# Latents' queries inside the expert stage's first tile, with groups of two choices and a ring of eight rows

## The chip, the cores and the metric

The kernel runs on one core of a Trainium2 chip. The metric is the device time of one execution in microseconds, as a median over several runs. The core has TensorE (PE, matmuls), VectorE (DVE), ScalarE (ACT), GpSimd (POOL, here the issuer of gathers) and SyncE (SP, the issuer of plain DMAs). Sixteen DMA engines carry all transfers.

## The reference

Two layers are applied to 128 context tokens and 512 latent tokens of width 1024. The part of a layer that the change touches is its last one, a retrieval of experts:

```python
def peer_ffn(h, lp):
    def chunk(hx):                                   # 128 tokens
        q = (hx @ wq).reshape(C, PEER_HEADS, 2, PEER_HALF)           # 8 heads, 2 x 64
        s = jnp.einsum('chpd,hpkd->chpk', q, sub_keys)               # 128 keys per half
        sv, si = lax.top_k(s, PEER_TOPK)                             # 16 best of each half
        comb = sv[:, :, 0, :, None] + sv[:, :, 1, None, :]
        fv, fi = lax.top_k(comb.reshape(..., 256), PEER_TOPK)        # 16 best pairs
        idx = e1 * PEER_N_KEYS + e2                                  # one of 16384 experts
        g = jax.nn.softmax(fv, axis=-1)
        u = jnp.take(u_tab, idx, axis=0)                             # a row of 1024
        act = jax.nn.gelu(jnp.einsum('chkd,cd->chk', u, hx))
        vv = jnp.take(v_tab, idx, axis=0)                            # a row of 1024
        return jnp.einsum('chk,chkd->cd', g * act, vv)
```

Its input `h` is the normed and modulated residual, and its result, times a gate, is added to the residual.

## The kernel before

A layer is a sequence of stages, each a block in which every engine runs its own instruction stream. A block ends when all its engines are done, so stages do not overlap. The tokens are five tiles of 128: tile 0 is the context, tiles 1 to 4 are the latents. The last three stages of a layer matter here.

**norm2** (`norm_stage`, lines 244 to 312) norms `x` and writes `h` transposed, features on partitions, as `t.h`.

**peer_query** (`peer_query_stage`, lines 1775 to 1870) does everything that leads to scores, for all five tiles. SP loads `peer_wq` in two DMAs of 2 MB and the keys (L1791, L1793). PE turns `h` back, tokens on partitions (L1820); DVE copies it and SP stores it in DRAM (`h_scratch`, L1796). PE multiplies with the query weights, per head once for the 128 context tokens and once for the 512 latents (L1829); ACT copies the queries (L1869). PE then makes the scores (L1841), DVE copies them (L1860), and SP stores them in DRAM as `score_scratch`, one DMA of 1 MB a tile (L1800).

**peer** (`peer_stage`, lines 1877 to 2086) runs over tile, head, and 16 choices. SP loads the scores of a head two heads ahead (L1912), and `h` at the start of a tile (L1921). DVE finds the 16 experts of a head (`look_up`, four pieces of five to eleven instructions: `scan`, `scan`, `combine`, `number_experts`), also two heads ahead. POOL issues one gather per choice (L1936): each of 128 partitions fetches one row of 8 KB (its `u` and `v`), 1 MB in all, into one of 16 buffers, the ring. DVE multiplies the `u` half with `h` and sums it (the dot, L2069), ACT applies Gelu (L1969), DVE multiplies with the softmax share (`weigh`, L2042), ACT makes a diagonal matrix of the 128 weights (L1973), and PE multiplies it with the `v` half and accumulates in two banks (mixing, L1948: 2 matmuls that the trace shows as 4 records). When PE has mixed a row, its buffer is free and POOL may issue the gather that uses it next: the gather of choice k waits for the mixing of choice k - 16.

DVE works in groups of four choices: four dots, then `weigh` of the group before, then a piece of the look-up. At the end of a tile ACT copies the sum (L1977) and DVE adds it to `x` one head later (L2047, L2049). The order is written by hand; only semaphores tie the engines.

## Time and profile before

| | us |
|---|---|
| median of 3 runs | 6662.83 |
| lowest and highest | 6654.68, 6679.47 |
| the profiled execution, time | 6667.52 |
| its span in the trace | 6665.8 |
| PE busy | 5361.1 (80%) |
| DVE busy | 3862.8 (58%) |
| ACT busy | 1258.8 (19%) |
| POOL busy | 1614.1 (24%) |
| granted TensorE clock, mean | 0.892 |

The span is one execution from its first to its last instruction. Busy shares are averages over stages with different limits. The page has 40 slices of the span, a chain of waits that ended last, and groups of instructions by line; the trace can be asked for windows, which give each engine's busy time in a stretch, and for the timeline.

### The profile page before, as it was taken

To read this page: it belongs to the slowest core of one execution; us is meant where nothing else is said; L and a number is where in the kernel's file an instruction comes from. 1 tells how busy PE (TensorE), PEld (TensorE's weight loads), DVE (VectorE), ACT (ScalarE), POOL (GpSimd) and SP (SyncE) were. 2 spreads that over 40 slices of the span, in tenths; PEclk is the share of its full clock that TensorE was granted. 3 is DMA by queue.
4 is the path that set the end of the run, shared out by engine and by line. 5 is a ranking of instruction groups with operands and counts; after the bars stand their busy time and mean duration, and the time that the engine had idled before them with its cause. 6 is when DMAs were issued, how large, how long until landed. Compare 5 with 4: busy or idle time off the path is not lost. (4 is left out here: it accounts for less than half of the span.)

```text
span 6665.8 us, 75292 instructions
## 1 busy us (share of the span) xinstructions
PE 5361.1 (80%) x25836; PEld 2849.1 (43%) x25836; DVE 3862.8 (58%) x8625; ACT 1258.8 (19%) x3092; POOL 1614.1 (24%) x1424
## 2 busy tenths in 40 slices
PE   7968899896677777778879688998957777777777
PEld 3545588454233333333335455884433333333333
DVE  2544666432767676767634445664337677767676
ACT  1022311101222121212111222111012222222221
POOL 0100000000444444444300000000004444444443
PEclk9978999898888889898889788998978888889998
DMA  3102601422999999999821026114239999999997
GB/s 118 65 35 88 241 28 48 156 94 96 419 419 419 419 415 413 409 410 408 330 105 62 35 101 228 37 38 176 75 117 419 419 420 419 415 415 408 410 411 321
DMA packets 330234, 1676.81 MB, mean 252 GB/s; under 512 B 36584, under 2 KB 71656, under 8 KB 164224
## 3 DMA queue, kind: packets, MB, share of 16 engines
q0 software_dynamic: 195296, 1377.52, 50.5%
q1 hardware_dynamic: 134560, 294.77, 12.2%
q8 instruction: 174, 2.85, 0.2%
q14 instruction: 204, 1.67, 0.1%
HBM read 1592.09 MB, written 80.08 MB: 251 GB/s over the span
## 5 line engine op out<-in xcount | busy, mean ns | idle before, releaser
L1948 PE MATMUL psum<-peer_rows,peer_diagonal 128*128 128x512 f32 x5120 | 2548.6, 659 | 841.4 <-ACT peer_diagonal L1973 834.4
L1936 POOL DMA_INDIRECT peer_rows<-in_peer_rows,peer_index x1280 | 1537.5, 1201 | 3450.0 <-DVE peer_best_at L1990 1725.1
L1948 PEld LDWEIGHTS psum<-peer_rows,peer_diagonal 128*128 128x128 f32 x5120 | 1062.1, 212 | 2326.6 <-issue 1295.7
L2069 DVE CUSTOM_DVE_ANT_0 peer_rows<-peer_rows,peer_h 128x1024 f32<-128x1024 f32 x1280 | 1546.8, 1225 | 795.8 <-DMA peer_rows<-in_peer_rows,peer_index 778.2
L1973 ACT ACTIVATE peer_diagonal<-ident_sb,peer_weight 128x128 f32<-128x128 f32 x1280 | 408.9, 390 | 2320.4 <-DVE peer_weight L2042 2299.0
L917 PE MATMUL psum<-h_sb,rw_in_gate_weights 128*128 128x128 f32 (+1 forms) x1024 | 286.2, 442 | 32.6 <-DMA rw_in_gate_weights<-in_w_gate 26.9
L448 PE MATMUL psum<-in_weights,h_sb 128*128 128x512 f32 (+1 forms) x800 | 309.5, 549 | 0.0
L894 POOL DMA_DIRECT2D rw_in_gate_weights<-in_w_gate x32 | 17.3, 542 | 944.2 <-DMA scratch_gate_scratch<-y_rw 720.0
L917 PEld LDWEIGHTS psum<-h_sb,rw_in_gate_weights 128*128 128x128 f32 x1024 | 160.0, 196 | 163.5 <-issue 128.8
L499 DVE SCALAR_TENSOR_TENSOR conv_acc<-conv_in,conv_taps,conv_acc 128x655 f32<-128x655 f32 x240 | 216.4, 902 | 8.5
L448 PEld LDWEIGHTS psum<-in_weights,h_sb 128*128 128x128 f32 x800 | 152.0, 190 | 158.1 <-issue 154.0
L1343 PE MATMUL psum<-wkv_inverse,wkv_inner 64*64 64x64 f32 x3200 | 195.0, 229 | 27.8 <-DVE wkv_inner L1537 27.7
L452 PE MATMUL psum<-h_sb,in_weights 128*128 128x128 f32 (+1 forms) x704 | 197.1, 444 | 20.9 <-DMA in_weights<-in_w_in 20.9
L1548 DVE TENSOR_TENSOR wkv_inverse<-wkv_inverse,psum 128x512 f32<-128x512 f32 (+1 forms) x200 | 123.8, 631 | 119.9 <-PE psum L1343 118.7
L1343 PEld LDWEIGHTS psum<-wkv_inverse,wkv_inner 64*64 64x64 f32 x3200 | 169.7, 144 | 36.0 <-DVE wkv_inner L1537 36.0
L1341 PE MATMUL psum<-wkv_inner,wkv_inverse 64*64 64x64 f32 x2560 | 173.7, 231 | 8.0 <-DVE wkv_inner L1537 7.9
L718 PE MATMUL psum<-h_sb,attention_gate_weights 128*128 128x128 f32 (+1 forms) x512 | 170.8, 479 | 0.0
L754 DVE COPY attention_probs_turned<-psum 128x512 f32<-128x512 f32 (+1 forms) x80 | 48.9, 612 | 205.6 <-PE psum L708 205.6
L452 PEld LDWEIGHTS psum<-h_sb,in_weights 128*128 128x128 f32 x704 | 110.2, 199 | 106.0 <-issue 84.6
L1341 PEld LDWEIGHTS psum<-wkv_inner,wkv_inverse 64*64 64x64 f32 x2560 | 147.2, 144 | 18.5 <-DVE wkv_inner L1537 9.4
L154 PE MATMUL psum<-rw_out_mod_weights,silu_sb 128*2 128x512 f32 x256 | 119.0, 620 | 31.5 <-DMA rw_out_mod_bias<-in_b_mod 31.5
L1829 PE MATMUL psum<-h_sb,query_weights 128*128 128x512 f32 (+1 forms) x512 | 140.7, 439 | 0.0
(331 smaller groups left out, 6087.6 us busy)
## 6 DMA issues: line engine op xcount, KB each, us to landing
rw_out_mod_weights<-in_w_mod SPq DMA_DIRECT2D x16, 2048.0 KB
in_weights<-in_w_in SPq DMA_DIRECT2D x12, 2048.0 KB, 8.5
peer_rows<-in_peer_rows,peer_index POOLq DMA_INDIRECT x1280, 18.2
modulation_weights<-in_w_mod SPq DMA_DIRECT2D x8, 2048.0 KB
rw_in_gate_weights<-in_w_gate POOLq DMA_DIRECT2D x32, 512.0 KB, 4.7
scratch_rw_scratch<-rw_in_direction SPq DMA_DIRECT2D x20, 768.0 KB, 4.6
wkv_own<-scratch_rw_scratch SPq DMA_DIRECT2D x20, 768.0 KB, 6.5
merge_gates<-scratch_gate_scratch SPq DMA_DIRECT2D x16, 960.0 KB
```

What stands on the lines that cost most here:

```text
L448: last = nc.tensor.matmul(t.bank[n % BANKS][:, 0:width(n)], t.h[:, k, i * P:(i + 1) * P], weights[c % 2][:, k, 0:chunks[c][1]], start=(k = ...
L452: last = nc.tensor.matmul(t.bank[n % BANKS][:, 0:m], weights[c % 2][:, k, i * P:(i + 1) * P], t.h[:, k, lo:lo + m], start=(k == 0), stop=( ...
L499: convolved.step(nc.vector.scalar_tensor_tensor(out=out, in0=t.conv_in[:, j, k:k + CONV_SPAN], scalar=taps[:, j, k:k + 1], in1=out, op0=AL ...
L718: last = nc.tensor.matmul(out, gate_weights[:, c, k, :], t.h[:, k, lo:lo + m], start=(k == 0), stop=(k == KD - 1))
L917: last = nc.tensor.matmul(out[:, 0:m], gate_weights[b % 2][:, k, :], t.h[:, k, lo:lo + m], start=(k == 0), stop=(k == KD - 1))
L1341: mm(banks(d)[1][rows, h * HB:(h + 1) * HB], inverse[n % 2][d][rows, 1, h, :], inner[d][rows, h, :], start=True, stop=True)
L1343: last = mm(banks(d)[1][rows, (4 + h) * HB:(5 + h) * HB], inner[d][rows, h, :], inverse[n % 2][d][rows, 1, h, :], start=True, stop=True)
L1829: last = nc.tensor.matmul(t.bank[4 + n % 4][:, 0:m], weights[h // 4][:, k, (h % 4) * P:(h % 4 + 1) * P], t.h[:, k, lo:lo + m], start=(k == ...
L1936: nc.gpsimd.indirect_dma_start(rows[k][:, :], None, t.dram["peer_rows"], bass.IndirectOffsetOnAxis(ap=index[j % 4][:, k:k + 1], axis=0)).t ...
L1948: last = nc.tensor.matmul(t.bank[c], diagonal[k % DIAGONALS][:, :], rows[k][:, D + c * 512:D + (c + 1) * 512], start=(j == 0 and k == 0), ...
L1973: nc.scalar.activation(diagonal[k % DIAGONALS][:, :], t.ident[:, :], ACT.Identity, scale=weight[b][:, k:k + 1]).then_inc(s["diagonal"], 1)
L2069: v.tensor_tensor_reduce(rows[k][:, 0:D], rows[k][:, 0:D], h[:, :], 1.0, 0.0, ALU.mult, ALU.add, dots[b][:, k:k + 1]).then_inc(s["dotted"], 1)
```

## The change

**Stages.** The query weights and keys are loaded during norm2. The peer_query stage handles only the context tile: queries, scores, turned rows. Its scores of heads 0 and 1 go straight to the buffers that the look-up reads; heads 2 to 7 are stored in DRAM in one DMA. Nothing of `h` goes through DRAM any more: `h_rows` is a tile in SBUF, rewritten by PE and ACT before each next tile. The latents' queries and scores are made inside tile 0 of the expert stage: one k-step of a head's query matmul ahead of each of the choices 0 to 7, and the scores of one latent tile ahead of each of the choices 8 to 11. ACT copies the query ahead of group 4 and the scores after the head; SP stores them, 512 KB a head.

**The expert stage.** The ring has 8 buffers instead of 16, so that the gather of choice k waits for the mixing of choice k - 8. Groups have two choices instead of four, `weigh` follows the dots of its own group (and, in every second group, the piece of look-up), and not those of the next. The sums of successive tiles alternate between two pairs of banks. Loops over tiles are written out, and the two look-ups beyond the last head are gone.

```diff
-def norm_stage(nc, t, s, before, which):
+def norm_stage(nc, t, s, before, which, layer):
...
+        if which:
+            @block.sync
+            def _(sp):
+                for c in range(2):
+                    sp.dma_start(t.query_weights[:, :, c * 512:(c + 1) * 512], ...).then_inc(s["query_loaded"], 16)
+                sp.dma_start(t.key_rows, ...).then_inc(s["query_loaded"], 16)
+                sp.wait_ge(s["query_loaded"], 48)
...
-    RING = 16
+    RING = 8
     DIAGONALS = 8
-    GROUP = 4
+    GROUP = 2
...
+            for n in range(TILES * HEADS):
+                if n + 2 < TILES * HEADS:
+                    sp.wait_ge(s["looked_up"], n + 1)
+                    if HEADS <= n + 2 < 2 * HEADS:
+                        sp.wait_ge(s["scores_stored"], 16 * (n + 3 - HEADS))
+                    sp.dma_start(scores[n % 2][:, :, :], t.dram["score_scratch"][n + 2, :, :, :]).then_inc(scores_loaded[n % 2], 16)
+                if 2 <= n < HEADS + 2:
+                    sp.wait_ge(s["scores_copied"], 2 * (n - 1))
+                    sp.dma_start(t.dram["score_scratch"][HEADS + n - 2:TILES * HEADS:HEADS, :, :, :]..., score_rows...).then_inc(s["scores_stored"], 16)
...
+            def latent_query(j, k):
+                if k == 0 and j:
+                    pe.wait_ge(s["query_copied"], j)
+                last = nc.tensor.matmul(query_bank, t.query_weights[:, k, j * P:(j + 1) * P], t.h[:, k, CTX:NTOK], start=(k == 0), stop=(k == KD - 1))
...
+            for i in range(TILES):
+                if i >= 2:
+                    pe.wait_ge(s["emptied"], i - 1)
                 for j in range(HEADS):
                     for k in range(TOPK):
+                        if i == 0 and k < KD:
+                            latent_query(j, k)
+                        if i == 0 and KD <= k < KD + TILES - 1:
+                            latent_scores(j, k - KD)
+                        if i < TILES - 1 and j == HEADS - 1 and 9 <= k < 13:
+                            turn_rows(i + 1, k - 9)
                         pe.wait_ge(s["diagonal"], (i * HEADS + j) * TOPK + k + 1)
...
                     for g in range(TOPK // GROUP):
+                        if i == 0 and g == 4:
+                            latent_query(j)
...
+                        if i < TILES - 1 and j == HEADS - 1 and g == TOPK // GROUP - 1:
+                            copy_rows(i + 1)
                         act.wait_ge(s["weighed"], n * (TOPK // GROUP) + g + 1)
                         for k in range(g * GROUP, (g + 1) * GROUP):
                             act.wait_ge(s["mixed"], n * TOPK + k + 1 + RING - DIAGONALS)
...
+                    if i == 0:
+                        latent_scores(j)
                 act.wait_ge(s["mixed"], (i + 1) * HEADS * TOPK + RING)
...
-                        if g:
-                            weigh(n, b, g - 1)
-                        look_up(g, done, n + 2, j + 2)
-                    weigh(n, b, TOPK // GROUP - 1)
+                        if g % 2 and n + 2 < TILES * HEADS:
+                            look_up(g // 2, done, n + 2, j + 2)
+                        weigh(n, b, g)
```

Three places show how the instructions move. The first is TensorE at the start of the expert stage's first head; before, behind the last score matmuls (L1841) and the block boundary, only mixing (L1948) stands there:

```order
L1841 MATMUL psum<-query_keys,query_queries 128x128 x80
L1777 UNCONDITIONAL_BRANCH
L1939 UNCONDITIONAL_BRANCH
L1942 UNCONDITIONAL_BRANCH
L1942 ISA
L1946 ISA
L1948 MATMUL psum<-peer_rows,peer_diagonal 128x512 x2
```

and now, from choice 6 on, query and score matmuls (L1929, L1939) stand between the mixing of two choices:

```order
L1929 MATMUL psum<-h_sb,query_weights 128x512
L1968 MATMUL psum<-peer_rows,peer_diagonal 128x512 x2
L1929 MATMUL psum<-h_sb,query_weights 128x512
L1968 MATMUL psum<-peer_rows,peer_diagonal 128x512 x2
L1939 MATMUL psum<-gate_rows_sb,peer_query 128x128 x2
L1968 MATMUL psum<-peer_rows,peer_diagonal 128x512 x2
```

A choice of tile 0 thus has up to one more 128x512 matmul ahead of its mixing; in the other tiles nothing is added but the turning of rows in the last head.

The second is VectorE at the start of a head. Before (`ISA peer_rows,peer_dots` is a dot, L2042 is `weigh`, L1989 begins a piece of the look-up):

```order
L2069 ISA peer_rows,peer_dots<-peer_rows,peer_h 128x1024
L2069 ISA peer_dots 128x1
L2069 ISA peer_rows,peer_dots<-peer_rows,peer_h 128x1024
L2069 ISA peer_dots 128x1
L2042 TENSOR_TENSOR peer_weight<-peer_active,peer_share 128x4
L1989 MAX peer_best<-peer_scores 128x8
L1990 MAX_INDEX peer_best_at<-peer_best,peer_scores 128x8
```

and now:

```order
L2111 ISA peer_rows,peer_dots<-peer_rows,h_rows 128x1024
L2111 ISA peer_dots 128x1
L2083 TENSOR_TENSOR peer_weight<-peer_active,peer_share 128x2
L2111 ISA peer_rows,peer_dots<-peer_rows,h_rows 128x1024
L2111 ISA peer_dots 128x1
L2111 ISA peer_rows,peer_dots<-peer_rows,h_rows 128x1024
L2111 ISA peer_dots 128x1
L2066 ISA
L2030 MAX peer_best<-peer_scores 128x8
```

The `weigh` before the look-up piece was that of the group before; now each `weigh` closes its own group.

The third is ScalarE over the middle of a head in tile 0. Before, a Gelu of four choices and four diagonals alternate:

```order
L1969 ACTIVATE peer_active<-peer_dots 128x4
L1973 ACTIVATE peer_diagonal<-ident_sb,peer_weight 128x128 x4
L1969 ACTIVATE peer_active<-peer_dots 128x4
L1973 ACTIVATE peer_diagonal<-ident_sb,peer_weight 128x128 x4
L1969 ACTIVATE peer_active<-peer_dots 128x4
```

and now they come by two, with the copy of the latents' query (L1976) between:

```order
L2006 ACTIVATE peer_active<-peer_dots 128x2
L2012 ACTIVATE peer_diagonal<-ident_sb,peer_weight 128x128 x2
L1976 COPY peer_query<-psum 128x512
L2006 ACTIVATE peer_active<-peer_dots 128x2
L2012 ACTIVATE peer_diagonal<-ident_sb,peer_weight 128x128 x2
```

The Gelu of choices 8 and 9 now stands behind a copy that waits for TensorE to finish the query.

## Rows read from the trace of the kernel before

**Rows 1.** The page: DMA busy tenths in forty slices, and the chain by line.

```profile
DMA  3102601422999999999821026114239999999997
...
DMA peer_rows<-in_peer_rows,peer_index 14%; PE psum L1948 5%; POOL peer_rows L1936 3%; DVE peer_rows L2069 0%; ACT peer_diagonal L1973 0%; POOLq L1934 0%; DVE peer_weight L2042 0%; DMA peer_iota<-in_iota 0%; POOLq L1935 0%; DVE peer_dots L2069 0%; DVE peer_out L2047 0%; DVE x_sb L2049 0%; ACTq L1972 0%; ACT peer_out L1977 0%; DVE peer_chosen L2010 0%
```

**Rows 2.** Windows: from:to, length, busy us by engine, PEclk, DMA share, GB/s.

```profile
1527.00:1545.80 18.80, 4.13 (x33) 3.45 (x33) 3.84 (x7) 0.00 (x0) 0.00 (x0) 0.73 0.83 308
1545.80:1618.50 72.70, 72.06 (x264) 41.10 (x264) 2.43 (x4) 6.82 (x16) 0.00 (x0) 0.97 0.06 22
1618.50:1643.70 25.20, 15.08 (x160) 14.88 (x160) 12.70 (x20) 0.00 (x0) 0.00 (x0) 0.82 0.66 219
...
1658.50:3309.60 1651.10, 1264.02 (x2528) 526.87 (x2528) 1184.23 (x2986) 342.86 (x954) 763.97 (x640) 0.88 1.00 411
...
4983.00:6634.60 1651.60, 1250.75 (x2528) 521.10 (x2528) 1184.55 (x2986) 342.86 (x954) 773.55 (x640) 0.89 1.00 411
```

**Rows 3.** Groups by line in the first layer's query stage.

```profile
L1829 PE MATMUL psum<-h_sb,query_weights 128*128 128x128 f32 (+1 forms) x256 | 70.3, 439 | 0.0
...
L1841 PE MATMUL psum<-query_keys,query_queries 64*128 64x128 f32 x160 | 15.1, 278 | 0.7 <-ACT query_queries L1869 0.7
```

**Rows 4.** DMA issues of the query stage: count, size, median us to landing.

```profile
query_weights<-in_peer_wq SPq DMA_DIRECT2D x4, 2048.0 KB, 11.7
...
scratch_score_scratch<-query_scores SPq DMA_DIRECT2D x10, 1024.0 KB, 4.8
...
query_keys<-in_peer_keys SPq DMA_DIRECT2D x2, 512.0 KB, 14.7
```

**Rows 5.** Timeline of norm2: its first instruction and its last group.

```profile
1508.36 1.06 ACT L264 ACTIVATE square<-x_sb 128x1024 f32<-128x1024 f32 x1 [88.91 <-PEq L1684]
...
1523.80 2.63 DVE L299 TENSOR_SCALAR h_sb<-psum,mod_sb 128x128 f32<-128x128 f32 x8
```

**Rows 6.** Timeline, expert stage's start: first issue, first gather, the fourth row's dot.

```profile
1643.74 0.35 SPq L1912 DMA_DIRECT2D peer_scores<-scratch_score_scratch  x1
...
1658.54 1.02 POOL L1936 DMA_INDIRECT peer_rows<-in_peer_rows,peer_index  x1 [862.57 <-DVE peer_best_at L1990]
...
1672.93 1.23 DVE L2069 CUSTOM_DVE_ANT_0 peer_rows<-peer_rows,peer_h 128x1024 f32<-128x1024 f32 x1 [0.99 <-DMA peer_rows<-in_peer_rows,peer_index]
```

**Rows 7.** Timeline of mixing in tile 1, and a gather that waited for it.

```profile
2258.01 9.53 PE L1948 MATMUL psum<-peer_rows,peer_diagonal 128*128 128x512 f32 x16 [4.63 <-ACT peer_diagonal L1973]
...
2308.86 7.13 PE L1948 MATMUL psum<-peer_rows,peer_diagonal 128*128 128x512 f32 x16 [0.40 <-ACT peer_diagonal L1973]
...
2311.66 1.75 POOL L1936 DMA_INDIRECT peer_rows<-in_peer_rows,peer_index  x1 [1.39 <-PE psum L1948]
```

**Rows 8.** Timeline at tile boundaries: a table load, a Gelu, a wait for h.

```profile
2008.59 1.28 ACT L1958 ACT_TABLE_LOAD   x1
...
2011.59 0.20 ACT L1969 ACTIVATE peer_active<-peer_dots 128x4 f32<-128x4 f32 x1
...
2329.97 0.16 DVE L2063 RECIPROCAL peer_inverse<-peer_total 128x1 f32<-128x1 f32 x1 [8.06 <-DMA peer_h<-scratch_h_scratch]
```

**Rows 9.** Timeline, end of the first layer's expert stage, by engine.

```profile
3307.14 1.22 DVE L2069 CUSTOM_DVE_ANT_0 peer_rows<-peer_rows,peer_h 128x1024 f32<-128x1024 f32 x1 [1.27 <-DMA peer_rows<-in_peer_rows,peer_index]
...
3309.62 1.23 DVE L2069 CUSTOM_DVE_ANT_0 peer_rows<-peer_rows,peer_h 128x1024 f32<-128x1024 f32 x1 [1.25 <-DMA peer_rows<-in_peer_rows,peer_index]
...
3310.77 0.16 DVE L2042 TENSOR_TENSOR peer_weight<-peer_active,peer_share 128x4 f32<-128x4 f32 x1
...
3314.36 0.16 DVE L2042 TENSOR_TENSOR peer_weight<-peer_active,peer_share 128x4 f32<-128x4 f32 x1
...
3311.04 1.28 ACT L1973 ACTIVATE peer_diagonal<-ident_sb,peer_weight 128x128 f32<-128x128 f32 x4 [9.55 <-DVE peer_weight L2042]
...
3328.54 1.01 ACT L1977 COPY peer_out<-psum 128x1024 f32<-128x1024 f32 x1 [12.62 <-PE psum L1948]
...
3311.49 17.01 PE L1948 MATMUL psum<-peer_rows,peer_diagonal 128*128 128x512 f32 x32 [3.79 <-ACT peer_diagonal L1973]
```

More of the change, by code:

```diff
@@ L1772, with peer_query_stage @@
          "projected", "sigmoid")
-def peer_query_stage(nc, t, s, before, layer):
+def peer_query_stage(nc, t, s, before):
     with ExitStack() as mem:
-        def sbuf(name, *shape):
-            return mem.enter_context(nc.sbuf_tensor("query_" + name, [P, *shape], F32))
-        weights = [sbuf(f"weights{b}", KD, 512) for b in range(2)]
-        keys, queries = sbuf("keys", HEADS, KEYS), sbuf("queries", HEADS, NTOK)
-        rows = [sbuf(f"rows{b}", D) for b in range(2)]
-        scores = [sbuf(f"scores{b}", HEADS, 2, KEYS) for b in range(2)]
+        queries = mem.enter_context(nc.sbuf_tensor("query_context", [P, HEADS, CTX], F32))
+        scores = mem.enter_context(nc.sbuf_tensor("query_scores", [P, HEADS, 2, KEYS], F32))
+        keys = t.key_rows.rearrange("p (h n) -> p h n", h=HEADS)
@@ L1834, in _, with score @@
[L1834 to L1835 removed]
+            def score(h):
+                pe.wait_ge(s["query_copied"], h + 1)
+                if h >= 2:
+                    pe.wait_ge(s["scores_copied"], 2 * (h - 1))
                 for c in range(2):
[L1837 to L1844 removed]
+                    nc.tensor.matmul(score_bank[2 * (h % 2) + c][:, 0:KEYS], queries[c * HD:(c + 1) * HD, h, :], keys[c * HD:(c + 1) * HD, h, :],
+                                     start=True, stop=True).then_inc(s["scored"], 1)
@@ L1846, in _ @@
+            query(0)
+            query(1)
+            score(0)
+            for half in range(2):
+                for k in range(4):
+                    last = nc.tensor.transpose(t.bank[half][:, k * P:(k + 1) * P], t.h[:, 4 * half + k, 0:CTX], t.ident[:, :])
+                last.then_inc(s["turned"], 1)
+            for h in range(2, HEADS):
+                query(h)
+                score(h - 1)
+            score(HEADS - 1)
         @block.vector
         def _(dve):
-            for i in range(TILES):
-                for half in range(2):
-                    dve.wait_ge(s["turned"], 2 * i + half + 1)
-                    if i >= 2:
-                        dve.wait_ge(stored[i % 2], 16 * (i // 2))
-                    nc.vector.tensor_copy(rows[i % 2][:, half * 512:(half + 1) * 512], t.bank[2 * (i % 2) + half][:, :]).then_inc(s["row_copied"], 1)
@@ new lines, in turn_rows @@
+            def turn_rows(i, part):
+                if part == 0:
+                    pe.wait_ge(s["query_copied"], HEADS)
+                    if i > 1:
+                        pe.wait_ge(s["row_copied"], 2 * (i - 1))
+                for k in range(2 * part, 2 * part + 2):
+                    last = nc.tensor.transpose(turned_banks[k // 4][:, k % 4 * P:(k % 4 + 1) * P], t.h[:, k, i * P:(i + 1) * P], t.ident[:, :])
+                if part % 2:
+                    last.then_inc(s["turned"], 1)
@@ L1976, in tile @@
                     act.wait_ge(s["added"], i)
-                nc.scalar.copy(out[:, :].rearrange("p (c n) -> p c n", c=2), t.psum[:, 0:2, :]).then_inc(s["emptied"], 1)
-            each_tile(act, tile)
+                nc.scalar.copy(out[:, :].rearrange("p (c n) -> p c n", c=2), t.psum[:, 2 * (i % 2):2 * (i % 2) + 2, :]).then_inc(s["emptied"], 1)
+            for i in range(TILES):
+                tile(i, i > 0)
         @block.vector
```

191 lines of the change are left out of this document (89 added, 102 removed).

## The prediction

> **What bounds the kernel now.** I read the page's slices first, then windows by stage, then the timeline of the stretches that the change touches. The slices show two plateaus where the DMA engines are busy at nine tenths or more [rows 1]: the expert stage of each layer. Windows put each at 1651 us, with a DMA share of 1.00 at 411 GB/s, against 76% for TensorE and 72% for VectorE [rows 2]. 640 gathers of 1.05 MB at 411 GB/s are 1633 us, so this stage goes at the pace of the gathers: the last rows land 2.5 us apart [rows 9], the mean is 2.57. The chain of waits is mostly gathers too [rows 1]. Nothing that shortens an engine's work there helps, and nothing that lengthens it hurts, as long as the next gather is issued in time. Ahead of it lies the query stage, where in 72.7 us TensorE works 72.1 and the DMA engines 6% [rows 2]. That is the work that the change moves under the gathers.
>
> **1. The query stage.** Before, from norm2's last write (1523.80 + 2.63 = 1526.4, [rows 5]) to the first gather (1658.54, [rows 6]) there are 132.1 us. Now the weights load under norm2: norm2 lasts 18.1 us [rows 5], and the loads land 11.7 and 14.7 us after their issue [rows 4], which hides them with some 2 us to spare. What TensorE keeps: query matmuls of 8 heads took 70.3 us for 640 tokens, so 14.1 for 128; scores of 40 pairs of head and tile took 15.1, so 3.0 for 8 [rows 3]; eight transposes, at most one head's context query, 1.8. That is 18.9 us at the higher clock. Wholly at the lower of the two levels it would be 38; since norm2's transposes come just before, I take 20. Then a last copy, score and copy (1.7, estimated), one store of 768 KB (1 MB landed in 4.8, [rows 4]; I take 4.8), two block boundaries (0.6 and 1.3, estimated), and the start of the expert stage, 14.8 us from SP's first issue to the first gather [rows 6], less 0.4 since the first score load is gone. Sum 20 + 1.7 + 4.8 + 1.9 + 14.4 = 42.8, **89 us less per layer**. Bounds: 71 (all at the lower clock) to 92.
>
> **2. The moved work in tile 0.** One choice costs TensorE 4 records of 7.13/16 = 0.446, or 1.78 us [rows 7], 28.5 a head. Added are 7.0 of queries and 1.5 of scores, together 37.0 in a head of 16 x 2.57 = 41.1. Over choices 0 to 7 it is 2.66 a choice, a lag of 0.7 us that choices 8 to 15 give back. The cover is DMA time. I cost it at **nothing**; wholly uncovered it would be 8 x 8.5 = 68 us a layer. ScalarE's copy of a query stands ahead of the Gelu of choices 8 and 9 and waits for TensorE's eighth k-step, and VectorE's `weigh` waits behind it; the row copies of the score at a head's end delay the next Gelu by 1.2. Both only lengthen the time that a row is held, which part 3 prices. SP's new stores are behind score loads that are needed two heads later.
>
> **3. The ring of eight.** Let H be the time from a row's landing to the end of its mixing. The gather that reuses its buffer is issued 1.0 us later (mixing from 2308.86, first row done 1.78 later, issue at 2311.66, [rows 7]). It lands no sooner than 6.9 us after that: the stage's fourth row landed at about 1672.9, the first 7.5 earlier, at 1665.4, its issue was at 1658.54 [rows 6]. Eight rows take 8 x 2.57 = 20.6 us, so the DMA engines stay fed while **H is at most 20.6 - 1.0 - 6.9 = 12.7 us**. Before, with sixteen, it was 33.
> A row of a pair waits 2.5 for its partner, then 1.15 for the last dot [rows 9]. With a look-up piece between dot and `weigh`, the longest is 3.6 (3310.77 to 3314.36), then 0.72 to TensorE (3310.77 to 3311.49, [rows 9]), then 1.78: H = 9.8. TensorE's clock: 16 records take 7.13 after an idle time of 0.40 and 9.53 after one of 4.63 [rows 7], so the first four or so run at 1.2 GHz; that adds up to 1.8, and H is 11.6. Choice 0, behind the longest piece and two table loads of 1.28 [rows 8], comes to 9.4. In tile 0, with queries ahead, I get 10 to 11.3. All are below 12.7, but by only 1 to 3 us. For occasional misses, POOL's longer issues (1.75 against 1.02, [rows 6, 7]) and the head in which VectorE adds to x, I take 6 us a layer (0 to 40).
> At a tile's end it is more. ScalarE has to wait until choice 15 is mixed: with choice 14 landing at 0, TensorE starts that pair at 8.1 and ends at 11.5 to 13.3. Then come the copy of the sum (1.01, [rows 9]), a table load, the exponential, a second table load (1.28 + 0.5 + 1.28, [rows 8]), and only then the Gelu of the new tile's first pair (0.20, [rows 8]) and 1.1 to TensorE, which was idle for 5 us and starts at the lower clock, 3.5 a row. That is 20.3 to 22.1 for a row that landed at 5.0: H = 15.3 to 17.1, or 2.6 to 4.4 over the limit. VectorE's old wait of 8.06 us for h [rows 8] cost nothing, since sixteen buffers covered it, so its removal gives nothing. Four boundaries at 3.5: **14 us more per layer**, between 0 and 18.
> The Trainium skill, DMA: Bandwidth & Descriptors, on the anatomy of one SWDGE DMA, gives a fixed 2.0 us plus the bytes at 436 GB/s, which is 4.4 us for such a gather. By that the limit for H would be 15.2, the boundaries would cost 1 us each, and the sum would be 20 us lower. The trace has 6.9 from the start of the issue, and I go by the trace.
>
> **4. Traffic.** Eight stores of 0.52 MB in 1 KB pieces are new. In the window of the old score stores 219 GB/s came at a share of 0.66 [rows 2], so 332 GB/s at full share, 1.6 us each, 12.6 in all; five loads of h (0.52 MB at 411 GB/s) are gone, 6.4. **6 us more per layer** (0 to 12).
>
> **5. The end.** From the last dot's start (3309.62) to ScalarE's copy (3328.54) there are 18.9 us, because the group of choices 8 to 11 was weighed only after the last dot and 32 records followed, 17.01 us [rows 9]. Now two rows are left: 2.5 us to TensorE, and 3.6 to 5.4 of mixing. **12 us less per layer** (11 to 13).
>
> **The sum.** -89 + 0 + 6 + 14 + 6 - 12 = -75 a layer, -150 for two. The profiled execution took 6667.5, 4.7 above the median: 6517.5, and against the median **6513 us**, 2.2% faster.
>
> **The rivals.**
> - The ring misses a little in every head: the 6.9 us are measured on idle DMA engines and may be 1 to 2 longer beside other transfers, so that choices 10 and 14 come late by 1 us. 80 heads, 80 us more: 6590. For it speaks the thin margin, against it that no gather in the old ring had to be that quick. 16%.
> - **Slower**: the ring of eight becomes the bound. With two rows at a time TensorE works 3.6 us and waits in each pair of 5.1. If these waits drop the clock in each turn, as the one of 4.63 did [rows 7], and the backlog is never worked off, H stays at about 14.6. Each of 160 turns of eight then costs 1.9 more, 304 in place of the 40 for part 3: 6777. It decides from H = 13.6 in every turn, where 0.94 x 160 = 150 eats the gain. Against it: such a TensorE would be busy without a gap, and within a busy stretch the trace's clock always rises (17.01 us for 32 records after 3.79 of idle, 14.3 of it if all were fast, [rows 9]). 10%. [...]
> - The move does not hide what it moves: TensorE in tile 0 falls behind by all that was added. 136 us: 6649. Against it is the 4 us of room in a head. 6%.
> - More gain: the boundaries and misses cost nothing, -95 a layer: 6473. It would need H at a boundary below 12.7 or a quicker landing. 8%.
>
> **How the numbers follow.** Forecast 60%, rivals 16, 10, 6 and 8. The range takes in the forecast, the small misses and the larger gain, with the bounds of parts 1 and 3: 6460 to 6620. Outside are the slower case and the uncovered move. What can be told from no change is 0.5%, or 33 us, so 6629 and 6696 are the limits: faster 0.84 (60 + 16 + 8), same 0.06 (the uncovered move), slower 0.10.
>
> **What the new profile would show.** From norm2's end to the first gather 40 to 46 us; the expert stage 1651 + 26 us to the last dot, with a DMA share of 1.00 but for a dip of some 3 us at each tile boundary; gathers landing 8 to 11 us after issue; GpSimd waiting for mixing, and VectorE still for gathers; the tail under 8 us. A stretch in ordinary heads where the DMA share falls below 0.95, or TensorE's clock under 0.8 in tiles 1 to 4, would say that the ring is the bound. A first tile longer than the others by over 10 us would say that the move is not covered. If landings come much sooner than 6.9 us, part 3 is too dear.

## The result and the profile after

The changed kernel takes **6462 us** (median of 4 runs, 6452.6 to 6467.2), beside 6663 us for the kernel before on the same chip: a ratio of 0.9694, interval 0.9672 to 0.9715. That is 201 us less (190 to 219 by the interval). Forecast were 150 us less and 6513 us. Set against the 6662.83 us of before, the ratio gives 6459 us, one below the range's lower end of 6460. The profiled execution took 6467.2 us (before: 6667.5).

The page's slices after, busy tenths and GB/s (as [rows 1]):

```profile
DMA  3201611333999999999931017113349999999999
GB/s 115 74 36 63 247 58 48 146 114 151 420 407 419 403 419 408 414 414 407 385 107 66 36 67 257 45 48 146 114 169 420 408 418 402 420 404 420 406 420 378
```

The plateaus are as high as before; what lay ahead of them is shorter. Windows after (from:to, length, busy us by engine, PEclk, DMA share, GB/s): the query stage's matmuls, its store and the expert stage's start, then the stretch from first gather to last dot in both layers, as [rows 2]:

```profile
1530.81:1551.88 21.07, 19.90 (x168) 18.05 (x168) 3.85 (x17) 3.24 (x11) 0.00 (x0) 1.00 0.01 2
1551.88:1569.30 17.42, 2.04 (x2) 0.50 (x2) 9.78 (x38) 1.52 (x3) 0.00 (x0) 0.56 0.14 46
1569.30:3222.56 1653.26, 1324.80 (x2837) 541.06 (x2838) 1194.49 (x3088) 420.37 (x1150) 711.96 (x640) 0.93 1.00 412
4794.96:6446.77 1651.81, 1314.74 (x2837) 537.76 (x2838) 1193.85 (x3089) 420.35 (x1150) 709.96 (x640) 0.93 1.00 412
```

The timeline after, from norm2's last write to the first gather (as [rows 5, 6]):

```profile
1528.17 2.64 DVE L308 TENSOR_SCALAR h_sb<-psum,mod_sb 128x128 f32<-128x128 f32 x8
...
1551.88 0.38 SPq L1796 DMA_DIRECT2D scratch_score_scratch<-query_scores  x1
1555.94 0.35 SPq L1899 DMA_DIRECT2D peer_iota<-in_iota  x1
...
1569.30 1.01 POOL L1920 DMA_INDIRECT peer_rows<-in_peer_rows,peer_index  x1 [775.64 <-DVE peer_index L2058]
```

and the end of the stage, as [rows 9]:

```profile
3219.74 3.70 PE L1968 MATMUL psum<-peer_rows,peer_diagonal 128*128 128x512 f32 x8 [1.28 <-ACT peer_diagonal L2012]
...
3222.56 1.22 DVE L2111 CUSTOM_DVE_ANT_0 peer_rows<-peer_rows,h_rows 128x1024 f32<-128x1024 f32 x1 [1.24 <-DMA peer_rows<-in_peer_rows,peer_index]
...
3228.45 1.01 ACT L2018 COPY peer_out<-psum 128x1024 f32<-128x1024 f32 x1 [3.50 <-PE psum L1968]
```

| per layer, us | before | after | difference | forecast |
|---|---|---|---|---|
| norm2's end to first gather (first layer; the second agrees within 0.2) | 132.1 | 38.5 | -93.6 | -89 |
| first gather to last dot (mean of two layers) | 1651.3 | 1652.5 | **+1.2** | **+26** |
| last dot to copy of the sum (mean of two layers) | 18.8 | 5.9 | -12.9 | -12 |

Twice the sum is -211, where the whole time fell by 201; the stages between differ by several us from run to run of any kernel. So two edges came out as forecast, and the plateau did not: 25 us a layer were expected there that never came. The experiments are about those 25.

**Where the boundaries went.** The stalls that the prediction saw at the tile boundaries are there. Windows of 15 us at the four boundaries of the changed kernel:

```profile
1920.00:1935.00 15.00, 13.22 (x26) 5.84 (x27) 11.82 (x34) 4.48 (x13) 6.77 (x6) 0.80 0.87 325
2250.00:2265.00 15.00, 13.32 (x25) 5.91 (x26) 11.87 (x35) 4.28 (x13) 5.96 (x5) 0.77 0.83 315
2580.00:2595.00 15.00, 14.32 (x29) 6.37 (x30) 12.59 (x35) 3.39 (x11) 7.36 (x6) 0.84 0.72 275
...
2910.00:2925.00 15.00, 14.98 (x28) 6.51 (x29) 12.48 (x36) 3.43 (x13) 6.93 (x6) 0.80 0.78 295
```

Against 419 GB/s in an undisturbed window these are 15 x (94 + 104 + 144 + 124) / 419 = 16.7 us of standing DMA engines. By their busy shares (0.87, 0.83, 0.72, 0.78) it is 12.0; 14 were forecast. But before, the same look at the later boundaries gives

```profile
2335.00:2365.00 30.00, 20.16 (x36) 8.50 (x37) 24.48 (x67) 7.42 (x21) 9.99 (x9) 0.78 1.00 407
2665.00:2695.00 30.00, 18.89 (x35) 7.96 (x36) 23.54 (x62) 7.29 (x20) 9.92 (x10) 0.80 0.94 377
2995.00:3025.00 30.00, 17.57 (x35) 7.13 (x33) 23.60 (x60) 7.51 (x18) 11.88 (x10) 0.81 0.98 387
```

which is 6 us lost there, and its stage ends strangely. The first rival was that sixteen buffers had not covered the old wait for h.

### The profile page after: what moved, and what is told of

Read it like the earlier page. It is cut to its first block and busy times, and to the rows that moved or that the text cites. A ratio compares the mean times of both kernels' runs of the same rounds, so it can differ in the third digit from the quotient of the medians.

```text
span 6465.5 us, 70198 instructions
## 1 busy us (share of the span) xinstructions
PE 5334.4 (83%) x25836; PEld 2787.7 (43%) x25836; DVE 3844.3 (59%) x8773; ACT 1402.2 (22%) x3456; POOL 1498.3 (23%) x1424
## 5 line engine op out<-in xcount | busy, mean ns | idle before, releaser
L1920 POOL DMA_INDIRECT peer_rows<-in_peer_rows,peer_index x1280 | 1421.9, 1111 | 3408.7 <-PE psum L1968 1809.6
L1968 PEld LDWEIGHTS psum<-peer_rows,peer_diagonal 128*128 128x128 f32 x5120 | 1005.3, 204 | 2130.4 <-issue 1132.5
L2111 DVE CUSTOM_DVE_ANT_0 peer_rows<-peer_rows,h_rows 128x1024 f32<-128x1024 f32 x1280 | 1549.7, 1223 | 606.1 <-DMA peer_rows<-in_peer_rows,peer_index 601.6
L2012 ACT ACTIVATE peer_diagonal<-ident_sb,peer_weight 128x128 f32<-128x128 f32 x1280 | 444.3, 394 | 819.1 <-DVE peer_weight L2083 815.0
L2006 ACT ACTIVATE peer_active<-peer_dots 128x2 f32<-128x2 f32 x640 | 130.4, 204 | 1535.2 <-DVE peer_dots L2111 1534.5
L2083 DVE TENSOR_TENSOR peer_weight<-peer_active,peer_share 128x2 f32<-128x2 f32 x640 | 102.3, 160 | 246.3 <-ACT peer_active L2006 238.3
L1352 PE MATMUL psum<-wkv_inverse,wkv_inner 64*64 64x64 f32 x3200 | 193.9, 229 | 27.7 <-DVE wkv_inner L1546 27.6
```

What stands on the lines that cost most here:

```text
L1352: last = mm(banks(d)[1][rows, (4 + h) * HB:(5 + h) * HB], inner[d][rows, h, :], inverse[n % 2][d][rows, 1, h, :], start=True, stop=True)
L1920: nc.gpsimd.indirect_dma_start(rows[spot][:, :], None, t.dram["peer_rows"], bass.IndirectOffsetOnAxis(ap=index[j % 4][:, k:k + 1], axis=0) ...
L1968: last = nc.tensor.matmul(t.bank[2 * (i % 2) + c], diagonal[k % DIAGONALS][:, :], rows[spot][:, D + c * 512:D + (c + 1) * 512], start=(j = ...
L2012: nc.scalar.activation(diagonal[k % DIAGONALS][:, :], t.ident[:, :], ACT.Identity, scale=weight[b][:, k:k + 1]).then_inc(s["diagonal"], 1)
L2111: v.tensor_tensor_reduce(rows[spot][:, 0:D], rows[spot][:, 0:D], h[:, :], 1.0, 0.0, ALU.mult, ALU.add, dots[b][:, k:k + 1]).then_inc(s["do ...
```

## The experiments

Stage lengths (first gather to last dot, us, both layers) are read from one traced execution of each kernel; its two layers mostly agree within 3 us, where whole times scatter by 10. A difference of under 2 us between two kernels is therefore not told from none. Each ratio is to the kernel before, timed beside it.

| run | stage, layer 1 / 2 | ratio, interval |
|---|---|---|
| before | 1651.1 / 1651.6 | 1 |
| h_early | 1651.6 / 1651.0 | 0.9996, 0.9987 to 1.0006 |
| g2_ring16 | 1650.1 / 1651.2 | 0.9960, 0.9946 to 0.9974 |
| g2_flat16 | 1644.7 / 1645.6 | 0.9955, 0.9938 to 0.9972 |
| g2_flat16_extra | 1653.8 / 1654.6 | 0.9976, 0.9966 to 0.9985 |
| stall1 | 1645.5 / 1645.2 | 0.9964, 0.9950 to 0.9979 |
| stall2 | 1661.0 / 1663.1 | 1.0008, 0.9998 to 1.0017 |
| g2_ring8 | 1665.3 / 1668.7 | 1.0024, 1.0014 to 1.0033 |
| flat8_h_early | 1654.0 / 1654.2 | 0.9978, 0.9968 to 0.9987 |
| changed kernel | 1653.3 / 1651.8 | 0.9694, 0.9672 to 0.9715 |
| late_copy | 1648.8 / 1647.8 | 0.9670, 0.9653 to 0.9686 |
| ring12 | 1646.9 / 1647.2 | 0.9663, 0.9647 to 0.9679 |
| both | 1647.2 / 1647.6 | 0.9668, 0.9652 to 0.9684 |
| extra_instr | 1658.2 / 1660.9 | 0.9711, 0.9695 to 0.9727 |
| stores2 | 1660.9 / 1665.2 | 0.9714, 0.9697 to 0.9730 |
| query2 | 1679.9 / 1680.3 | 0.9775, 0.9759 to 0.9791 |
| ring7 | 1691.2 / 1685.7 | 0.9791, 0.9775 to 0.9808 |

**1. The old wait for h.** From the kernel before:

```diff
+                    if j == 2 and i + 1 < TILES:
+                        sp.wait_ge(s["tile_done"], i + 1)
+                        sp.dma_start(h_next[:, :], t.dram["h_scratch"][(i + 1) * P:(i + 2) * P, :]).then_inc(s["h_loaded"], 16)
...
+                v.tensor_copy(h[:, :], h_next[:, :]).then_inc(s["tile_done"], 1)
```

SyncE's loop over tiles is written out as well, and to make room for `h_next` three scratch tiles of the look-up share memory.

> The kernel before, with h of the next tile loaded into a second buffer during the tile and copied by VectorE at the tile's start (about 1 us), instead of a load of 8 us that VectorE waits for. By the prediction the old wait was covered by sixteen buffers: no change, 6663 us, the windows around tile boundaries as before. Rival (the old wait was not covered in the later tiles, where the trace of before has 10-us windows of 335 to 396 GB/s): 3 to 5 us less at each of the later boundaries, 10 to 20 us less per layer, 6625 to 6645 us, and the dips after the boundaries gone.

No change, in the stage or in all. The first rival falls: the prediction's "sixteen buffers covered it" stands.

**2. Groups of two and the ring, apart.** g2_ring16 has only this; g2_ring8 has `RING = 8` as well.

```diff
-    GROUP = 4
+    GROUP = 2
...
-                        if g:
-                            weigh(n, b, g - 1)
-                        look_up(g, done, n + 2, j + 2)
-                    weigh(n, b, TOPK // GROUP - 1)
+                        if g % 2:
+                            look_up(g // 2, done, n + 2, j + 2)
+                        weigh(n, b, g)
```

> The kernel before with groups of two choices, each weighed behind its own dots, and nothing else; the ring stays at sixteen. By the prediction only the end gets shorter, by 12 us a layer: 6639 us, time from last dot to copy 6 to 7 us, the stretch from the first gather to the last dot 1651 us as before. Rival (groups of four themselves cost DMA time, through later releases): the stretch gets shorter too, by 5 us or more.

> The same with a ring of eight: the change without its move of queries and without h rows in SBUF. By the prediction a ring of eight costs 20 us a layer for boundaries and misses, and here the 8 us of loading h are uncovered as well, 4 x 3 to 5 more: 32 to 40 a layer over the kernel with sixteen, so 6700 to 6720 us. Rival A (a landing takes under 6 us, so that eight rows are enough but for the boundaries): 15 to 25 a layer, 6670 to 6690 us. Rival B (sixteen rows have a cost of their own, a DMA engine that lags and ends 9 us after the others): the stage ends with all engines together, and the ring costs under 10 a layer, below 6660 us.

Groups of two leave the stage as it was (1650.6 against 1651.3) and shorten the end. The whole time fell by 25 us, 17 to 36 by the interval, where 24 were expected, but the end itself took 9.1 and 12.1 us in the two layers and not the 6 to 7 expected: 9.8 and 6.6 less, 16 in all. With the stages' 1.4 that makes 18 us, at the low end of the interval. What holds the end up is a piece of look-up beyond the last head, which stands between the last dot and its `weigh` here and is gone in the changed kernel (in the first layer):

```profile
3303.01 1.23 DVE L2069 CUSTOM_DVE_ANT_0 peer_rows<-peer_rows,peer_h 128x1024 f32<-128x1024 f32 x1 [1.26 <-DMA peer_rows<-in_peer_rows,peer_index]
...
3307.69 0.16 DVE L2042 TENSOR_TENSOR peer_weight<-peer_active,peer_share 128x2 f32<-128x2 f32 x1
...
3312.15 1.01 ACT L1977 COPY peer_out<-psum 128x1024 f32<-128x1024 f32 x1 [3.50 <-PE psum L1948]
```

It takes 3.4 us there, so some 3 of the changed kernel's 12.9 us at the end come from the dropped look-ups.

The ring of eight costs 16.4 us a layer with the wait for h uncovered, half of the 32 to 40 expected: rival A's size. What explained the size was seen in the stage's end. Windows of g2_ring16:

```profile
3278.00:3280.00 2.00, 2.00 (x6) 0.77 (x5) 1.39 (x3) 0.34 (x2) 0.00 (x0) 1.00 1.03 434
...
3282.00:3284.00 2.00, 2.00 (x5) 0.57 (x3) 0.93 (x1) 0.00 (x0) 0.00 (x0) 1.00 0.19 78
...
3288.00:3292.00 4.00, 4.00 (x6) 1.56 (x6) 2.63 (x5) 0.90 (x3) 0.00 (x0) 0.57 0.06 27
...
3296.00:3300.00 4.00, 1.84 (x3) 0.81 (x4) 3.66 (x10) 0.77 (x3) 0.00 (x0) 0.80 0.06 25
```

A share of 0.06 is one engine of sixteen, and 27 GB/s is its full pace (419 / 16 = 26). It works alone for 17 us, from 3286 to the last dot at 3303 (two others end at about 3286, the middle ones at 3282), with the last gathers waiting for its part. Before, the same lasts 9 us:

```profile
3296.00:3298.00 2.00, 2.00 (x6) 0.95 (x5) 1.23 (x2) 0.00 (x0) 0.00 (x0) 1.00 1.04 430
3298.00:3300.00 2.00, 1.25 (x3) 0.19 (x1) 1.31 (x4) 0.00 (x0) 0.00 (x0) 1.00 0.62 258
3300.00:3302.00 2.00, 1.43 (x4) 0.72 (x5) 1.86 (x7) 1.37 (x5) 0.00 (x0) 1.00 0.07 29
...
3306.00:3308.00 2.00, 1.70 (x4) 0.39 (x3) 0.86 (x1) 0.00 (x0) 0.00 (x0) 1.00 0.07 29
```

and in the changed kernel all end within 2 us (share 0.97, then 0.17):

```profile
3218.00:3220.00 2.00, 0.72 (x3) 0.26 (x2) 0.98 (x3) 0.90 (x3) 0.00 (x0) 1.00 0.97 401
3220.00:3222.00 2.00, 2.00 (x6) 0.80 (x6) 1.23 (x2) 0.00 (x0) 0.00 (x0) 1.00 0.17 70
```

**3. The changed kernel without its boundary stalls.**

```diff
+                        if i and j == 0 and g == 1:
+                            copy_sum(i - 1)
...
+            def copy_sum(i):
...
+            copy_sum(TILES - 1)
```

> The changed kernel with ScalarE's copy of a tile's sum moved behind the second group of the next tile, so that the next head's exponential and Gelu no longer wait for the last mixing. By the prediction a boundary costs 3.5 us, four in a layer: 14 us less per layer, ratio to the kernel before 0.965 in place of 0.969, and no window under 400 GB/s at the boundaries 0 to 1 up to 3 to 4. Rival (the boundaries cost nothing in the sum, what is lost there comes back): no change, ratio 0.969.

Windows of late_copy at the same four boundaries:

```profile
1905.00:1920.00 15.00, 12.00 (x27) 4.59 (x25) 9.36 (x24) 5.37 (x14) 7.85 (x8) 1.00 1.02 420
2240.00:2255.00 15.00, 11.27 (x22) 4.42 (x20) 8.81 (x24) 3.28 (x10) 6.48 (x6) 0.83 1.02 421
2565.00:2580.00 15.00, 12.02 (x27) 4.97 (x26) 10.59 (x32) 3.59 (x10) 7.31 (x7) 0.92 0.99 396
2895.00:2910.00 15.00, 12.09 (x28) 4.77 (x26) 9.86 (x27) 4.03 (x12) 7.23 (x7) 1.00 1.00 406
```

Of 16.7 us of standing only 1.2 are left, by the same sum (by the shares nothing; the next 10 us behind the second window have 346 to 359 GB/s at shares of 0.97 to 0.99), and the stage is 4.2 us shorter. So of the 12 to 15 us that went, some 8 to 11 had cost nothing. The new theory (so called in the expectations below): one DMA engine has more to do than the rest, the stage ends when that one is done, and a stall in which it still works off a backlog is free.

**4. A pause of known length.** g2_flat16 (below) has the ring of sixteen and a lone engine for 19 us at its end. stall1 and stall2 add to it, ahead of one head of the last tile in each layer, a pause in the issue of gathers:

```diff
+                    if i == 4 and j == 2:
+                        for n in range(100):        # 200 in stall2
+                            nc.gpsimd.memset(idle[:, :], 0.0).then_inc(s["idled"], 1)
+                            pool.wait_ge(s["idled"], n + 1)
```

> The kernel g2_flat16 (ring of sixteen) with 100 small memsets, one after the other, on GpSimd ahead of the gathers of one head in the last tile, a pause in the issue of gathers of some 15 to 25 us. The lone engine lags behind the others by some 16 us at that point, and a gather lands 31 us after its issue. New theory (a pause shorter than the lagging engine's backlog costs nothing, whatever the other fifteen lose): a dip in GB/s where the fifteen run dry, 1645 us from first gather to last dot as without it, and at the stage's end a lone engine for less than 19 us, shorter by the dip. By the prediction's reckoning (what the DMA engines stand still is lost): longer by the dip.

> The same with 200 memsets, a pause of twice the length. New theory: only what the pause has over the 31 us to landing is lost, so between 0 and 20 us in each layer, some 15 us less than the fifteen engines stand still, and no lone engine is left at the end. By the prediction's reckoning: the whole dip is lost.

GpSimd's timeline in stall1 has the pause from 3023.95 to 3045.69, 21.7 us, and its windows show what the DMA engines did meanwhile and at the end:

```profile
3025.00:3030.00 5.00, 4.49 (x12) 2.06 (x12) 3.75 (x8) 1.59 (x5) 3.65 (x24) 1.00 1.01 415
3030.00:3035.00 5.00, 3.34 (x9) 1.31 (x8) 4.12 (x13) 0.90 (x3) 3.64 (x24) 1.00 0.55 228
3035.00:3040.00 5.00, 5.00 (x13) 2.08 (x12) 2.64 (x6) 0.90 (x3) 3.63 (x25) 1.00 0.06 26
3040.00:3045.00 5.00, 1.54 (x4) 0.38 (x2) 4.08 (x13) 0.20 (x1) 3.54 (x24) 0.90 0.06 26
3045.00:3050.00 5.00, 4.37 (x5) 1.85 (x6) 3.83 (x8) 1.59 (x5) 3.70 (x3) 0.50 0.48 146
...
3286.00:3288.00 2.00, 2.00 (x6) 0.76 (x4) 1.93 (x6) 0.20 (x1) 0.00 (x0) 1.00 1.01 414
3288.00:3292.00 4.00, 1.51 (x4) 0.68 (x4) 3.83 (x12) 0.69 (x2) 0.00 (x0) 1.00 0.59 244
3292.00:3296.00 4.00, 4.00 (x10) 1.71 (x9) 1.99 (x5) 0.90 (x3) 0.00 (x0) 1.00 0.06 23
```

Fifteen engines stand for about 15 us (5 x 191 + 5 x 393 + 5 x 393 + 5 x 273 over 419), the sixteenth works on at 26 GB/s, the stage is as long as without the pause (1645.3 against 1645.1), and at its end the lone engine needs some 4 us instead of 19. In stall2 (42.7 us of pause) the lone engine runs dry as well:

```profile
3049.00:3054.00 5.00, 3.94 (x5) 1.65 (x6) 4.19 (x10) 1.59 (x5) 3.64 (x24) 0.66 0.07 25
3054.00:3059.00 5.00, 4.89 (x12) 1.90 (x10) 2.80 (x8) 0.20 (x1) 3.65 (x24) 1.00 0.01 5
...
3064.00:3069.00 5.00, 1.04 (x3) 0.19 (x1) 0.00 (x0) 0.59 (x1) 3.63 (x25) 0.84 0.00 0
```

and the stage is 16.9 us longer, about what the lone engine stood (3055 to 3071, but for one score load), where the others stood over 30. So a stall within the lone engine's backlog was free, and one beyond it cost what that engine lost.

**5. What burdens that engine.** g2_flat16 is g2_ring16 with the loops over tiles written out on all engines, as in the changed kernel:

```diff
-            with pe.Fori(0, TILES) as i:
+            for i in range(TILES):
```

g2_flat16_extra and extra_instr (from the changed kernel) add, behind each score load,

```diff
+                    for _ in range(150):
+                        sp.sem_inc(s["spare"], 1)
+                    sp.sem_clear(s["spare"])
```

> The kernel before with groups of two (as g2_ring16, ring of sixteen), and the expert stage's loops over tiles written out, which changes how instructions are fetched but no work. New theory: one of the sixteen DMA engines has more to do than the others, because it also fetches instructions (0.61 MB in an expert stage, 24 us at 25.7 GB/s), and the stage ends when that one is done: in g2_ring16 a single engine works for 19 us after the others. Written out, the changed kernel fetched 0.34 MB over that queue and 0.36 over another, so here 8 to 10 us less per layer, 1640 to 1642 us from first gather to last dot, a lone engine for about 9 us at the end, 6625 us in all. By the prediction, where all engines end together and stalls alone cost time: no change against g2_ring16, 1650 us, 6641 in all.

> The kernel g2_flat16 (ring of sixteen, groups of two, loops written out) with 150 semaphore increments more behind every score load on SyncE, some 365 KB of instructions a layer. There a lone DMA engine works for 19 us at the stage's end, so it has no idle time in which these could hide. New theory (that engine is the one that fetches them, 14 us for 365 KB at 25.7 GB/s): 10 to 14 us more per layer, 1655 to 1659 us from first gather to last dot, 6655 to 6662 in all, more than the 7 a layer in the ring of eight. If they fall on another engine: no change, 1645 us and 6634.

> The changed kernel with 150 semaphore increments more behind every score load on SyncE, an engine that mostly waits: 5700 instructions a layer, 365 KB at 64 bytes each, and no other work. New theory (an engine's instruction fetches hold up the gathers on one DMA engine): up to 14 us more per layer where they fall on the fullest one, 6475 to 6490 us; less than 3 a layer would mean that they fall on another one. By the prediction: no change, 6462 us.

The DMA view of the stage (queue, packets, MB, share) has for g2_ring16, g2_flat16, g2_flat16_extra and the changed kernel, in this order:

```profile
q14 instruction: 76, 0.62, 0.1%
```
```profile
q14 instruction: 50, 0.41, 0.1%
```
```profile
q14 instruction: 97, 0.79, 0.1%
```
```profile
q14 instruction: 42, 0.34, 0.1%
```

26 packets fewer gave 5.5 us less, 47 more gave 9.1 more: on average 0.2 us a packet of 8 KB, in stages where the lone engine never rests. In the ring of eight 45 more gave 7.0. The direction is as expected, the size 0.6 of it, and g2_flat16's lone engine still works 19 us, not 9: the fifteen others are done earlier by as much. The fetched bytes did not fall in g2_flat16: a second queue, q8, went from 4 to 20 packets of 16 KB.

That packets fall on this very engine is not only concluded from the time. The trace records when each of the sixteen engines raises a gather's semaphore. For each gather take the last of the sixteen landings, which late in the stage is the lone engine's, and the eighth, and the time from one gather's to the next one's. The median is 2.49 us for both. The table counts the intervals longer than that by over 0.6 us, and how many of these have the start of a q14 packet in them or within 1 us ahead, in the first layer:

| run | intervals, with a packet | last landing: long ones, with a packet | eighth: long ones, with a packet |
|---|---|---|---|
| g2_ring16 | 639, 85 | 34, 30 | 10, 6 |
| both (experiment 6) | 639, 50 | 26, 23 | 9, 2 |
| g2_flat16_extra | 637, 110 | 55, 48 | 15, 7 |

The long ones with a packet are longer by 0.98 us in the median (0.75 in g2_flat16_extra). So some 40 to 55% of the packets fall on the last engine and cost it about 1.0 us each, far more than the 0.2 us that all packets cost on average. In g2_ring16 the last landings take 20.7 us more from first to last than the eighth ones (1644.2 against 1623.5), and the 30 long intervals add up to 34.7 us against 5.4 for the eighth: the fetches are enough to account for the whole lag. A likely part of what g2_flat16 saves stands there too, not tested by itself: with loops, two tile boundaries (2647 to 2655 and 2979 to 2986) have 5 packets within 8 us and delay the last landing by 4.3 us each, and written out no 8 us have more than two.

The Trainium skill, Runtime: NRT & Kernel Launch, on instruction fetch mechanics, says that each engine's sequencer fetches blocks of instructions by a DMA queue of its own, mostly hidden; here, where a DMA engine is the bound, it isn't. The Trainium skill, DMA: Bandwidth & Descriptors, on latency and other measured facts, says that two of the sixteen engines are usually slower, for an uncertain cause. The landings here show one far behind and two behind by less, without their numbers, and the one far behind moves at the common pace of 2.49 us between the fetches; why so many fetches meet that engine stays open.

**6. The ring.** ring12 and ring7 are the changed kernel with one number changed; both has `copy_sum` moved as well. flat8_h_early is g2_flat16 with a ring of eight and the early h of h_early.

```diff
-    RING = 8
+    RING = 12        # 7 in ring7
```

> The changed kernel with a ring of twelve: the limit for the time that a row is held rises from 12.7 to 23 us, above all that the prediction has at a tile's end (15.3 to 17.1). By the prediction boundaries and misses go: 20 us less per layer, 1633 us from first gather to last dot, 6422 in all. New theory (the fullest DMA engine catches up while the others stand still, so most of a stall costs nothing): 3 to 8 us less per layer, 1645 to 1649 us, 6447 to 6456 in all, and a lone engine at the stage's end for several us.

> The changed kernel with a ring of seven: 2.57 us less for a row to be held. By the prediction (issue to landing at least 6.9 us, a row held for 9.8 to 11.6 us in ordinary heads) the limit falls to 10.1 us and most turns of seven come late by up to 1.5 us: some 0.75 x 91 turns, 70 us more per layer with the boundaries, 6600 in all. Rival (a gather can land in 5.6 us, the least seen in the changed kernel, and the limit is 11.4): ordinary heads just keep up, only boundaries cost 2.6 more each, 10 to 20 us a layer, 6485 to 6500 in all.

> The kernel before with groups of two, loops written out, a ring of eight and h of the next tile loaded a tile ahead and copied by VectorE: the changed kernel's stage but for the work and traffic that it moves into the first tile. New theory: 1645 for ring sixteen (g2_flat16) plus 4 to 6 for eight buffers (ring12 against the changed kernel) gives 1649 to 1651 us from first gather to last dot, 6645 in all; the moved stores then account for the rest up to 1652.5. By the prediction the ring costs 20: 1665 us, 6674 in all.

> The changed kernel with a ring of twelve and with the copy of a tile's sum moved behind the second group of the next tile: the two edits that gave 4 to 6 us a layer each. New theory (below some 1645 us the stage cannot come, since one DMA engine is busy all the time): no sum of the two, 1644 to 1647 us from first gather to last dot, 6440 in all. By the prediction (stalls alone): 8 to 10 us less per layer than the changed kernel, 1643 us, or down to 1633 if all stalls go.

Twelve buffers give 5.5 us a layer, not 20, and both edits together no more than one of them (1647.4): under some 1645 us the lone engine is the floor. By itself, beside g2_flat16, a ring of eight costs 8.9 us. Ring 7 costs 35.9, between the prediction's 70 and the rival's 10 to 20. The times from issue to landing (min, median, max) of the changed kernel and of ring7:

```profile
DMA to landing us min/median/max: 5.6/11.2/15.4
```
```profile
DMA to landing us min/median/max: 5.5/9.1/14.6
```

The least is 5.5, not the 6.9 of the prediction, so the limit for a held row is about 14 us at eight buffers and 11.5 at seven. That is in the midst of the 9.8 to 11.6 that the prediction reckoned for a held row; how long rows were held was not measured.

**7. Traffic and the moved work.** stores2 and query2, from the changed kernel:

```diff
+                    sp.dma_start(t.dram["spare_scratch"][HEADS + n - 2:TILES * HEADS:HEADS, :, :, :]..., score_rows...).then_inc(s["scores_stored"], 16)
```
```diff
+                nc.tensor.matmul(t.bank[5], t.query_weights[:, k, j * P:(j + 1) * P], t.h[:, k, CTX:NTOK], start=(k == 0), stop=(k == KD - 1))
```

> The changed kernel with each of the eight score stores of the first tile done twice (the second time to a spare place in DRAM). By the prediction a store costs 1.6 us: 12.6 us more per layer, 1665 us from first gather to last dot, 6487 in all. Rival (the stores fill time that is lost anyway): under 5 us a layer, below 6472. By its bytes alone at the stage's own pace (4.2 MB at 411 GB/s) it would be 10.

> The changed kernel with each of the latents' query matmuls issued twice in the first tile (the second into a bank that nobody reads). TensorE then has 37 + 7 = 44 us of work in a head of the first tile, against 41 to 42.4 between heads. By the prediction the move is covered by DMA time with some 4 us a head to spare: 2 to 3 us more in each of 8 heads, 16 to 28 a layer, 1668 to 1680 us from first gather to last dot, 6495 to 6520 in all. If the moved work already cost time, the whole of the added 7 us a head would show: 56 a layer, 6575.

4.2 MB cost 10.5 us: their bytes at the stage's pace, less than the 1.6 us a store of the prediction. A doubled query costs 27.6 us, all of it in the first tile (from its first gather to the next tile's 361 against 330 us, of which the second tile gives 3 back): 3.4 a head, as 44 us of work against 41 to 42 demand, and at the upper end of what was expected. So the move itself was covered, with little to spare.

## Why the prediction was wrong

- **What bounds the kernel**: right that the stage goes at the gathers' pace, wrong in what that pace is. It took the DMA engines as one, by their mean share of 1.00 [rows 2]. The bound is one of the sixteen.
- **Part 1, query stage, -89**: right, -93.6, though 1.6 beyond its own bound of 92. From norm2's end to the last copy and store issue 21.1 us (22.3 forecast, the boundary of 0.6 with it), TensorE busy 19.9 at a granted clock of 1.00; store and boundary 4.1 (6.1); the start 13.4 (14.4). norm2 was not lengthened by the loads.
- **Part 2, nothing**: right (query2), TensorE has little spare in the first tile.
- **Part 3, +20, the step that failed.** Its chain of events was right: the boundary stalls are there, 12 us of standing by the shares and 16.7 by the bytes, where 14 were forecast. The failed step is "four boundaries at 3.5: 14 us more": it priced a stall at its length. late_copy values them at 4.2, and the smaller ring as a whole costs 5.5 (against ring12) to 8.9 (flat8_h_early) where 20 were forecast. The limit of 12.7 us was too strict as well, by the 6.9 us to landing, where 5.5 is the least seen. The 6.9 were reckoned back from the fourth row in steps of 2.5; in the changed kernel the stage's first gather landed 5.6 us after its issue and the second 3.3 us behind it. The 6 us for misses are not to be seen apart. The clock was taken to add up to 1.8 us to a pair; the two rows it was read from differ by 9.53 - 7.13 = 2.4. The Trainium skill, DMA: Bandwidth & Descriptors, on the anatomy of one SWDGE DMA, would put the landing at 4.4 us, an estimate from its 2.0 us and the bytes at 436 GB/s; no trace here shows so quick a landing.
- **Part 4, +6**: the doubled stores give 10.5 for eight; less the 6.4 of the old loads about 4 by this estimate. Beside flat8_h_early the changed kernel's first tile is 9.0 us longer (330.4 against 321.4 from gather to gather, first layer) and the four others together 10.9 shorter, so the traffic is there, and something at the later tiles, not tested by itself, gives more back.
- **A part not costed at all**: the loops written out. The prediction has no term for them; they take 5.5 us off the stage (g2_flat16).
- **Part 5, -12**: right, -12.9. Groups of two alone (g2_ring16) gave 9.8 and 6.6 of it in the two layers; the rest needed the last look-ups to be gone.
- **The rivals.** "More gain" came true (8% had been given) and for its stated reason only in part: H at a boundary was not below the limit, landing was quicker, and most of a stall was free. The slower rival fell: pairs of mixing take 3.70 us for 8 records after 1.28 of idle, and the stage's granted clock rose from 0.88 to 0.93. Small misses in every head did not come at eight buffers; at seven they did.

Closed, the stage per layer goes: 1651.3 before; -0.7 groups of two; -5.5 loops written out; +8.9 ring of eight, with h loaded early; -1.5 for the rest (h turned on the chip, moved work, net traffic), which makes 1652.5. Against the forecast of +26 the 25 us that never came are thus 11 in the ring (8.9 for 20), 5.5 in the loops, 7.5 in traffic and the rest (-1.5 for +6), and 0.7 in the groups; the last and the -1.5 are within what one trace can tell. Twice (+1.2 - 26) is -50 us of the difference to the forecast, and the two edges give -11 more. The whole time differs from the forecast by 51 and not by 61; the other 10 us lie in the stages between, whose times scatter by several us from run to run.

The same runs hold a faster kernel: late_copy, ring12 and both take 6442 to 6444 us, a ratio of 0.966 to 0.967. Against the changed kernel's 0.9694 the intervals overlap, but the stages are 4 to 6 us shorter in each layer. The three can't be told apart, and by the whole times alone they are not shown to beat the changed kernel.

## What to carry to other kernels

A mean DMA share of 1.00 does not say that all sixteen engines are needed all the time: look at the last 20 us of the stage in windows of 2 us, and if the share falls to 0.06 while one engine goes on, that engine is the bound, and stalls shorter than its backlog are free. Price a stall by what the bounding engine loses in it, not by its length, and when a ring is made smaller, ask first whether the depth bought anything but a longer lead of the fast engines. In a stage bound by DMA the instructions of all engines are traffic too: here a packet of 8 KB cost the bounding engine about 1.0 us where it fell on it, and the stage 0.2 us on average.

## What the runs showed of the hardware

- Of the sixteen DMA engines that share each gather, one was behind at the stage's end when the ring had sixteen buffers: by 17 us in g2_ring16, 19 in g2_flat16 and 9 in the kernel before, after 1650 us. With eight buffers it was under 2.
- In the kernel before the mean rate was 419 GB/s in the second tile, 414 in the third and 409 to 410 in the last two.
- 5700 to 6000 semaphore increments on an engine that mostly waits cost 7 to 9 us a layer, by their fetching alone as far as the traces show.
- The last landing of a gather came 2.49 us behind that of the gather before, and 3.47 where an instruction packet fell on the lone engine (g2_ring16).
- A gather of 1 MB landed 5.5 us after its issue at the least, while others were in flight (ring7), and 5.6 as the first of a stage (changed kernel).
- Loops over tiles moved instruction bytes from one queue to another: 76 and 4 packets with loops became 50 and 20 written out, those of the second queue twice as large.
